# Transformer kernel of split products: an operand's high part first, two norms reordered, a copy moved ahead of a split, the experts' end rotated and halved

## The chip, the cores and the metric

The kernel runs on one core of a Trainium2 chip. The metric is the time of the device for one execution, in microseconds; the shown time is the median of three runs. Everything is float32 data.

## What is computed

Two transformer blocks run over 256 positions of width 1024. The first has a convolution and gated linear attention mixer and a convolutional MLP. The second has two layers: stick-breaking and "fox" attention with a SwiGLU of 2816 columns, then sliding-window attention with a mixture of eight experts, top two of eight for each position. Each of the two layers ends with a gated embedding term. Cut to the parts that the change touches:

```python
x = x + rmsnorm(mixer(rmsnorm(x, g0)), g1)          # w_in ... w_out
h = rmsnorm(x, g2)                                  # two norms in a row after w_out
x = x + rmsnorm(conv_mlp(h), g3)                    # w_up, w_down
x = layer_norm(ALPHA * x + fox_sb_mixer(x))         # ab_in, ab_out
x = layer_norm(ALPHA * x + swiglu(x))               # ffn_up, ffn_down
x = x + sigmoid(x @ ple_gate[0]) * (p[0] @ ple_proj[0])
x = layer_norm(ALPHA * x + swa_mixer(x))            # qkv, c_out
combine = top2_softmax(x @ router_w + router_b)
y = sum(combine[:, e] * swiglu_e(x) for e in range(8))   # 44 weight chunks for each expert
x = layer_norm(ALPHA * x + y)
x = x + sigmoid(x @ ple_gate[1]) * (p[1] @ ple_proj[1])
```

## The kernel before

All five engines follow programs written out by hand, tied by counting semaphores. PE (TensorE) multiplies, ACT (ScalarE) and DVE (VectorE) prepare operands, SP issues the weight loads, POOL some small loads.

**Split products.** A float32 product is made of three: high times high, high times low, low times high. A weight chunk of 128 rows x 2048 columns is loaded to `w_raw`; ACT rounds it to `w_hi` (L611), DVE subtracts to `w_lo` (L1138, in the experts L1701). `w_hi` and `w_lo` have four slots (`RING`). `round_to(c)` on ACT and DVE does all chunks up to number c, so its place in a program sets when a chunk is made. PE waits for `lo_ready` before a chunk and reports `w_used` after it.

**Operands.** Between two projections `operand(m, src)` on PE turns the new activations: it waits for `t_source` of tile 0 (128 positions), makes eight transposes (L1996), then the same for tile 1. ACT rounds each half tile to `xt_hi`, DVE subtracts to `xt_lo` (L1150). Between the steps PE multiplies constants (`keep_warm`, L2001), whose results nobody reads. Their numbers stand in tables; after tile 1 there are seven, and then PE waits for all four pieces of `xt_lo`:

```python
                if m not in (6, 10):
                    keep_warm(7, 3)
                pe.wait_ge(S("xt_ready"), 4 * (m + 1))
```

`cols_chunk` (L1976 to L1979) and `rows_chunk` (L1922 to L1924) then make the three products of each 128 rows of a chunk, one after the other. `operand` serves w_up (m = 2), ab_in (3), ffn_up (5), qkv (7) and the router (9).

**After w_out.** Two norms follow each other: `rms_after` (L1210 to L1218) adds to x, `rms_before` (L1187 to L1195) makes y for w_up. Both go tile by tile: both norms of tile 0, then both of tile 1. ACT takes the squares, the roots, and the `xt_hi` copies in the same order.

**Sliding-window attention.** For each of eight pairs of heads, PE turns the weights, DVE copies them out (`turned_prob`, L1449), PE multiplies by the values (`swa_pv`, L2413 to L2415). Ahead of the last copy DVE splits a weight chunk of c_out (`round_to(c_sw + 7)`) and two pieces of `xt_lo`.

**Experts.** `item(i)` runs expert i: 28 chunks up, 16 down, the latter in two halves of 512 columns (n = 0, 1). ACT and DVE make `ys_hi`, `ys_lo` of a half (L1759), PE's `scatter` (L2485, eight products) puts both halves back to the positions at the start of the next item, and DVE adds them to y (`added`, L1716, a tile of 1024 columns each). The programs of ACT and DVE run two chunks ahead of PE, and end an item with the first four chunks of the next; behind the last expert these are the four chunks of the last embedding term (ple1: two of 1024 columns, which these instructions treat as 2048, and two of 2048). Only then each engine tests whether more than eight items are needed (`overflow`, a nest of `If`); here eight are. DVE then adds, takes the statistics (L1892) and normalizes (L1234 to L1241) tile 0, and PE turns it.

## Time and profile before

| what | value |
|---|---|
| median of three runs (range) | 1875.41 us (1875.24 to 1876.05) |
| profiled execution, its own time | 1876.83 us |
| its span, first to last instruction | 1874.7 us |
| PE busy / DVE busy / ACT busy | 97% / 74% / 59% |
| chain that ended last: PE / DVE / ACT | 87% / 7% / 2% |
| mean granted clock of TensorE | 0.991 |

The span holds the stages w_in to w_down (up to 341 us), the first layer of the second block (to 708), qkv and its attention (to 786), c_out and the router (to 822), the eight experts (to 1826) and the last embedding term. PE's busy share counts the constant products too, so an idle PE is only a part of what a late operand costs: what counts is when the first product with data starts.

### The profile page before, as it was taken

The numbers are of one execution on the slowest core, as the hardware profiler recorded it, in microseconds if no ns is written. First come the engines' busy times: TensorE is split into PE (matmuls) and PEld (weight loads), VectorE is DVE, ScalarE is ACT, GpSimd is POOL, SyncE is SP. The second block draws the span as 40 slices with busy tenths as digits, with TensorE's granted clock in tenths as the row PEclk, the third lists the DMA queues.
The fourth block names the chain that finished last, engine by engine and source line by source line (L and its number), as shares of the span: only waits on it lengthen the run. The fifth ranks groups of instructions, "written<-read, shape, count | busy, mean of one in ns | idle before, by whom it ended". The sixth has DMA issues, their size and how long they took to land.

```text
span 1874.7 us, 24092 instructions
## 1 busy us (share of the span) xinstructions
PE 1827.1 (97%) x9840; PEld 1527.8 (81%) x9849; DVE 1388.8 (74%) x1200; ACT 1105.0 (59%) x989; POOL 61.6 (3%) x83
## 2 busy tenths in 40 slices
PE   8999999999999999999999999999999999999997
PEld 6979997897899877768788888888888888888875
DVE  4766775456655565689988888888888888888876
ACT  4544554364343344367766676767666767676672
POOL 2200000200000001000000000000000000000000
PEclk8999999999999999999999999999999999999998
DMA  7444546432555563259999999999999999999980
GB/s 252 158 153 157 179 157 213 141 131 100 176 179 179 179 203 136 69 205 384 339 381 361 338 368 352 362 356 342 377 361 340 366 355 362 356 342 379 357 308 24
DMA packets 248857, 491.02 MB, mean 262 GB/s; under 512 B 10423, under 2 KB 15611, under 8 KB 248753
## 3 DMA queue, kind: packets, MB, share of 16 engines
q1 hardware_dynamic: 244992, 477.30, 72.0%
q0 software_dynamic: 3328, 10.73, 1.7%
q8 instruction: 69, 1.13, 0.3%
q10 hardware_dynamic: 432, 1.57, 0.2%
q14 instruction: 36, 0.29, 0.0%
HBM read 487.46 MB, written 2.10 MB: 261 GB/s over the span
## 4 chain that ended last, share of the span: by engine, by line
PE 87%; DVE 7%; ACT 2%; issue 1%; DVEq 1%; DMA 0%; ACTq 0%; SPq 0%
PE psum L2511 17%; PE psum L2513 17%; PE psum L2512 17%; PE psum L1976 5%; PE psum L1979 5%; PE psum L1978 5%; PE psum L1922 5%; PE psum L1923 5%; PE psum L1924 5%; PE psum L1996 3%; DVE w_lo L1138 2%; ACT w_hi L611 1%; DVE w_lo L1701 1%; DVE uv L1398 1%; PE psum L2485 1%
## 5 line engine op out<-in xcount | busy, mean ns | idle before, releaser
L611 ACT ACTIVATE w_hi<-w_raw 128x2048 fp32r<-128x2048 f32 (+1 forms) x357 | 641.4, 1834 | 106.7 <-PE psum L1924 60.3
L1701 DVE TENSOR_TENSOR w_lo<-w_raw,w_hi 128x2048 fp32r<-128x2048 f32 (+1 forms) x238 | 511.3, 2187 | 75.2 <-ACT w_hi L611 75.0
L1138 DVE TENSOR_TENSOR w_lo<-w_raw,w_hi 128x2048 fp32r<-128x2048 f32 (+2 forms) x119 | 261.3, 2227 | 138.9 <-ACT w_hi L611 137.5
L2511 PE MATMUL psum<-w_hi,xg_hi 128*128 128x512 f32 x892 | 357.7, 401 | 1.3 <-DVE w_lo L1701 1.3
L2513 PE MATMUL psum<-w_hi,xg_lo 128*128 128x512 f32 x892 | 353.5, 396 | 0.0
L2512 PE MATMUL psum<-w_lo,xg_hi 128*128 128x512 f32 x892 | 353.5, 396 | 0.0
L1701 DVE TENSOR_TENSOR w_lo<-raw_more,w_hi 128x2048 fp32r<-128x2048 f32 (+1 forms) x118 | 254.5, 2195 | 35.2 <-ACT w_hi L611 35.0
L1976 PE MATMUL psum<-xt_hi,w_hi 128*128 128x256 f32 (+1 forms) x976 | 277.0, 284 | 0.7 <-DVE w_lo L1138 0.7
L1978 PE MATMUL psum<-xt_lo,w_hi 128*128 128x256 f32 (+1 forms) x976 | 274.8, 282 | 0.0
L1979 PE MATMUL psum<-xt_hi,w_lo 128*128 128x256 f32 (+1 forms) x976 | 274.8, 282 | 0.0
L611 ACT ACTIVATE w_hi<-raw_more 128x2048 fp32r<-128x2048 f32 (+1 forms) x118 | 212.7, 1838 | 19.0 <-PE psum L2513 18.5
L2511 PEld LDWEIGHTS psum<-w_hi,xg_hi 128*128 128x128 f32 x892 | 168.1, 188 | 40.9 <-DVE w_lo L1701 2.2
L2513 PEld LDWEIGHTS psum<-w_hi,xg_lo 128*128 128x128 f32 x892 | 167.9, 188 | 40.8
L2512 PEld LDWEIGHTS psum<-w_lo,xg_hi 128*128 128x128 f32 x892 | 168.2, 189 | 38.5
L1976 PEld LDWEIGHTS psum<-xt_hi,w_hi 128*128 128x128 f32 (+1 forms) x976 | 181.8, 186 | 3.5 <-DVE w_lo L1138 1.5
L1978 PEld LDWEIGHTS psum<-xt_lo,w_hi 128*128 128x128 f32 (+1 forms) x976 | 182.6, 187 | 0.5
L1979 PEld LDWEIGHTS psum<-xt_hi,w_lo 128*128 128x128 f32 (+1 forms) x976 | 182.6, 187 | 0.3
L2511 PE MATMUL psum<-w_hi,mh_hi 128*128 128x512 f32 x448 | 179.1, 400 | 0.0
L2513 PE MATMUL psum<-w_hi,mh_lo 128*128 128x512 f32 x448 | 177.6, 397 | 0.0
L2512 PE MATMUL psum<-w_lo,mh_hi 128*128 128x512 f32 x448 | 177.4, 396 | 0.0
L611 ACT ACTIVATE mg<-psum 128x512 f32<-128x512 f32 x56 | 33.6, 599 | 176.1 <-PE psum L2513 176.1
L1922 PE MATMUL psum<-w_hi,xt_hi 128*128 128x512 f32 (+1 forms) x256 | 104.5, 408 | 5.2 <-DVE xt_lo L1150 3.7
(395 smaller groups left out, 2122.9 us busy)
## 6 DMA issues: line engine op xcount, KB each, us to landing
w_raw<-in_moe_w_gate_up SPq DMA_DIRECT2D x150, 1024.0 KB, 7.8
raw_more<-in_moe_w_gate_up SPq DMA_DIRECT2D x74, 1024.0 KB, 7.7
w_raw<-in_moe_w_down SPq DMA_DIRECT2D x64, 1024.0 KB, 7.2
raw_more<-in_moe_w_down SPq DMA_DIRECT2D x32, 1024.0 KB, 7.5
w_raw<-in_w_up SPq DMA_DIRECT2D x22, 1024.0 KB, 5.4
w_raw<-in_ffn_w_gate_up SPq DMA_DIRECT2D x22, 1024.0 KB, 5.4
w_raw<-in_w_in SPq DMA_DIRECT2D x12, 1024.0 KB, 5.6
w_raw<-in_ab_w_in SPq DMA_DIRECT2D x12, 1024.0 KB, 5.2
```

What stands on the lines that cost most here:

```text
L611: return act.activation(o, i, func, **kw)
L1138: TT(w_lo[:, k % RING, 0:n], raw(slot, n), w_hi[:, k % RING, 0:n].bitcast(F32), ALU.subtract)\
L1701: TT(w_lo[:, at, 0:n], raw(slot, n), w_hi[:, at, 0:n].bitcast(F32), ALU.subtract).then_inc(S("lo_ready"), 1)
L1922: mm(o, hi(k, t), wh, start=(k == ps[0][0]), stop=False)
L1923: mm(o, hi(k, t), wl, start=False, stop=False)
L1924: m = mm(o, lo(k, t), wh, start=False, stop=(k == kmax))
L1976: mm(o, w_hi[:, slot, cols], xt_hi[:, k, :], start=(k == 0 and c_ % 2 == 0), stop=False, skip_group_check=True)
L1978: mm(o, w_hi[:, slot, cols], xt_lo[:, k, :], start=False, stop=False, skip_group_check=True)
L1979: m = mm(o, w_lo[:, slot, cols], xt_hi[:, k, :], start=False, stop=(k == KD - 1), skip_group_check=True)
L2511: mm(o, hi[:, q, :], wh, start=(q == first), stop=False)
L2512: mm(o, hi[:, q, :], wl, start=False, stop=False)
L2513: m = mm(o, lo[:, q, :], wh, start=False, stop=(q == last))
```

## The change

- `operand` makes two constant products behind tile 1 instead of seven and no longer waits for `xt_lo`. The first chunk of the projection behind it multiplies the high part first (`cols_chunk_high_first` for w_up, ab_in and ffn_up, `rows_operand_high_first` for qkv, the router's loop likewise), and waits for `xt_lo` before the last third. For this the router's scores and the turned embedding of layer 0 (`p_bank`) use other banks.
- After w_out, ACT and DVE do the first norm of both tiles, then the second norm of both. Between the two tiles PE makes 5 constant products, not 14.
- In the attention, the last `turned_prob` stands ahead of the split of the c_out chunk, and the next split moves behind `attended`.
- `item` is cut into `item_head` and `item_end`. Behind the last expert the test for more items comes ahead of the four ple1 chunks on ACT and DVE. `scatter` and `added` go by halves of columns, not by tiles: PE puts half 0 back ahead of the test, half 1 behind it; seven constant products there go, and six in ple1. DVE makes only the two 1024-column chunks ahead of the sum, the other two later.
- `ple(1)` uses `rows_high_first`: both chunks' products with `w_hi` for tile 0, then the turning of tile 1, then those with `w_lo`.

```diff
-            return psum[:, 2 * (phase["c_out"][0][0] % 2), :] if i else scr[:, 3, :]
+            return psum[:, 2 * (phase[("ab_out", "c_out")[i]][1 - i][0] % 2), :]
+        def logit_bank():
+            return psum[0:N_EXP, 2 * (phase["c_out"][1][0] % 2), 0:SEQ]
...
             for t in squares("w_out"):
-                if t == 1:
-                    for j in range(2):
-                        turned(2, j)
                 root_tile(t)
+            for t in range(NT):
                 square_x(t, y, lambda t: act.wait_ge(S("x_tile"), t + 1))
                 root_tile(t)
+            for j in range(2):
+                turned(2, j)
...
+                end = MOE_UP_CHUNKS + len(MOE_DOWN)
+                rounds(k, end + 2, i)
+                wait_used(act, c0 + end, r)
+                item_rows(0)
+                rounds(end + 2, MOE_CHUNKS, i)
+            def item_rows(n):
+                copy(ys_hi[:, n * NB:(n + 1) * NB], psum[:, 4 + n, :], scale=gslot[:, 0:1]).then_inc(S("ys_hi_ready"), 1)
+            def item_end(i):
+                rounds(MOE_CHUNKS, MOE_CHUNKS + 2, i)
+                wait_used(act, N_BEFORE_MOE, (i + 1) * R_ITEM)
+                item_rows(1)
+                rounds(MOE_CHUNKS + 2, MOE_CHUNKS + 4, i)
+            def last_end():
+                c0 = chunk0["ple1"]
+                round_to(c0 + 2, n_items * R_ITEM)
+                wait_used(act, N_BEFORE_MOE, n_items * R_ITEM)
+                item_rows(1)
+                round_to(c0 + 4, n_items * R_ITEM)
...
                 n_items = act.value_load(route_i[0:1, 3:4], min_val=N_EXP, max_val=ITEMS)
-                for i in range(1, N_EXP):
+                n_over = act.value_load(route_i[0:1, 4:5], min_val=0, max_val=ITEMS - N_EXP)
+                for i in range(1, N_EXP - 1):
                     item(i)
+                item_head(N_EXP - 1)
                 def overflow(i):
                     with act.If(n_items > i):
-                        item(i)
+                        item_end(i - 1)
+                        item_head(i)
                         if i + 1 < ITEMS:
                             overflow(i + 1)
                     act.end_ifs()
                 overflow(N_EXP)
                 me.cap = N_STATIC
+                last_end()
                 root_tile(0)
             if "ple1" in live:
...
             for t in rms_after(1, "w_out", "x_tile"):
+                pass
+            for t in range(NT):
                 rms_before(t, 2)
             dve.sem_inc(S("gain_used"), 1)
...
                 if i:
-                    round_to(blocks[0][1] + RING, r)
                     turned(m, 0)
                     turned(m, 1)
                     normalize(1, m, y)
                     dve.sem_inc(S("gain_used"), 2)
+                    round_to(blocks[0][1] + 3, r)
                     turned(m, 2)
                     turned(m, 3)
+                    round_to(blocks[0][1] + 4, r)
                 else:
                     round_to(blocks[0][1] + 4, r)
                     turned(m, 2)
...
                 turned_prob(6)
                 swa_sink(1)
-                round_to(c_sw + 7)
                 for t in range(NT):
                     turned_at(8, t, 2 * t, scr[:, t, :])
                 turned_prob(7)
-                round_to(c_sw + 8)
+                round_to(c_sw + 7)
                 attended(1)
                 for t in range(NT):
...
-            def added(n, t):
-                dve.wait_ge(S("scattered"), 2 * n + t)
-                TT(y[:, t, :], y[:, t, :], psum[:, 4 + 2 * t:6 + 2 * t, :].rearrange("p b n -> p (b n)"), ALU.add)\
-                    .then_inc(S("y_added"), 1)
+            def added(n, h, tiles=range(NT)):
+                dve.wait_ge(S("scattered"), 2 * n + h)
+                cols = slice(h * NB, (h + 1) * NB)
+                for t in tiles:
+                    i = TT(y[:, t, cols], y[:, t, cols], psum[:, 4 + 2 * t + h, :], ALU.add)
+                return i
             def scattered(n):
-                for t in range(NT):
-                    added(n, t)
+                for h in range(2):
+                    added(n, h).then_inc(S("y_added"), 1)
+            def add_last(t):
+                added(n_items, 1, (t,))
+                dve.bn_stats(bn[:, t, 0, :], y[:, t, 0:NB])
+                dve.drain()
+                dve.bn_stats(bn[:, t, 1, :], y[:, t, NB:D])
             def item(i, first=False):
+                item_head(i, first)
+                item_end(i)
+            def item_head(i, first=False):
...
+            def last_end():
+                round_to(chunk0["ple1"] + 2, n_items * R_ITEM)
+                dve.wait_ge(S("ys_hi_ready"), 2 * n_items)
+                item_rows(1)
...
+                last_end()
+                added(n_items, 0)
+                dve.drain()
                 add_last(0)
                 normalize(0, 10, y)
                 add_last(1)
...
+            def cols_chunk_high_first(bl, i, r, m_):
+                bb, cc, n0, n, ps = bl
+                k0, nk, _ = ps[i]
+                slot = (cc + i) % RING
+                pe.wait_ge(S("lo_ready"), RING + cc + i + 1 + RING * r)
+                pe.wait_ge(S("xt_hi_ready"), 4 * m_ + (3 if k0 + nk <= 4 else 4))
+                for part in range(2):
+                    if part:
+                        pe.wait_ge(S("xt_ready"), 4 * (m_ + 1))
+                    for kk in range(nk):
+                        k = k0 + kk
+                        for c_ in range(-(-n // P)):
+                            w_ = min(P, n - c_ * P)
+                            cols = slice(kk * n + c_ * P, kk * n + c_ * P + w_)
+                            o = acc_t(bb % 2, c_)[0:w_, :]
+                            if part:
+                                m = mm(o, w_hi[:, slot, cols], xt_lo[:, k, :], start=False, stop=(k == KD - 1), skip_group_check=True)
+                            else:
+                                mm(o, w_hi[:, slot, cols], xt_hi[:, k, :], start=(k == 0 and c_ % 2 == 0), stop=False,
+                                   skip_group_check=True)
+                                mm(o, w_lo[:, slot, cols], xt_hi[:, k, :], start=False, stop=False, skip_group_check=True)
+                m.then_inc(S("w_used"), 1)
...
-            BETWEEN = (0, 4, 14, 9, 4, 13, 4, 2, 4, 11, 4)
+            BETWEEN = (0, 4, 5, 9, 4, 13, 4, 2, 4, 11, 4)
...
-                if m not in (6, 10):
-                    keep_warm(7, 3)
-                pe.wait_ge(S("xt_ready"), 4 * (m + 1))
+                keep_warm(2, 3)
...
-            def up(blocks, r):
-                for b_ in blocks:
+            def up(blocks, r, m=2):
+                products_t(blocks[0], r, m)
+                if m == 5:
+                    pe.wait_ge(S("ppt_ready"), 1)
+                for b_ in blocks[1:]:
...
-                for b_ in (ks_b, qs_b):
-                    products_t(b_, 0)
+                products_t(ks_b, 0, 3)
+                products_t(qs_b, 0)
...
+                high(0, 0)
+                high(1, 0)
+                turn_tile(m, src, 1)
+                low(0, 0)
+                pe.wait_ge(S("xt_ready"), 4 * m + 4)
+                high(0, 1)
+                high(1, 1)
+                low(0, 1).then_inc(S("w_used"), 1)
+                low(1, 0)
+                low(1, 1).then_inc(S("w_used"), 1)
...
-                    pe.wait_ge(S("y_added"), 2 * n_items + 2)
-                    keep_warm(6)
...
-                products(kv_b, 0, xh, xl)
+                wait_acc(kv_b[0])
+                rows_operand_high_first(kv_b, 7)
...
-            def scatter(n):
-                pe.wait_ge(S("ys_ready"), 2 * n)
-                for t in range(NT):
-                    for h in range(2):
-                        for q, part in enumerate((ys_hi, ys_lo)):
-                            m = mm(psum[:, 4 + 2 * t + h, :], selt[:, t * P:(t + 1) * P], part[:, h * NB:(h + 1) * NB],
-                                   start=(q == 0), stop=(q == 1))
-                    m.then_inc(S("scattered"), 1)
+            def scatter(n, h):
+                pe.wait_ge(S("ys_ready"), 2 * n - 1 + h)
+                for t in range(NT):
+                    for q, part in enumerate((ys_hi, ys_lo)):
+                        m = mm(psum[:, 4 + 2 * t + h, :], selt[:, t * P:(t + 1) * P], part[:, h * NB:(h + 1) * NB],
+                               start=(q == 0), stop=(q == 1))
+                m.then_inc(S("scattered"), 1)
...
+                o = logit_bank()
                 for k in range(KD):
-                    o = scr[0:N_EXP, 0, 0:SEQ]
+                    if k % 4 == 0:
+                        pe.wait_ge(S("xt_hi_ready"), 4 * 9 + 3 + k // 4)
                     mm(o, rw_hi[:, k, :], xt_hi[:, k, :], start=(k == 0), stop=False)
-                    mm(o, rw_hi[:, k, :], xt_lo[:, k, :], start=False, stop=False)
-                    m = mm(o, rw_lo[:, k, :], xt_hi[:, k, :], start=False, stop=(k == KD - 1))
+                    mm(o, rw_lo[:, k, :], xt_hi[:, k, :], start=False, stop=False)
+                pe.wait_ge(S("xt_ready"), 4 * 9 + 4)
+                for k in range(KD):
+                    m = mm(o, rw_hi[:, k, :], xt_lo[:, k, :], start=False, stop=(k == KD - 1))
...
-                keep_warm(7, 0)
-                scatter(N_EXP)
+                scatter(N_EXP, 0)
                 def overflow(i):
                     with pe.If(n_items > i):
                         item(i)
+                        scatter(i + 1, 0)
                         if i + 1 < ITEMS:
                             overflow(i + 1)
-                        if i == N_EXP:
-                            scatter(n_items)
                     pe.end_ifs()
                 overflow(N_EXP)
+                scatter(n_items, 1)
             if "ple1" in live:
```

DVE around the two norms after w_out (x is written by the first norm, y by the second). Before:

```order
L1218 SCALAR_TENSOR_TENSOR x<-y,stat,x 128x1024
L1187 TENSOR_SCALAR stat<-stat 128x1
L1178 RECIPROCAL stat<-stat 128x1
L1195 SCALAR_TENSOR_TENSOR y<-x,stat,gain 128x1024
L1210 TENSOR_TENSOR stat<-stat 128x1
L1187 TENSOR_SCALAR stat<-stat 128x1
L1214 TENSOR_TENSOR y<-psum,gain 128x512
L1178 RECIPROCAL stat<-stat 128x1
L1218 SCALAR_TENSOR_TENSOR x<-y,stat,x 128x1024
```

and now:

```order
L1245 SCALAR_TENSOR_TENSOR x<-y,stat,x 128x1024
L1237 TENSOR_TENSOR stat<-stat 128x1
L1214 TENSOR_SCALAR stat<-stat 128x1
L1241 TENSOR_TENSOR y<-psum,gain 128x512
L1205 RECIPROCAL stat<-stat 128x1
L1245 SCALAR_TENSOR_TENSOR x<-y,stat,x 128x1024
L1214 TENSOR_SCALAR stat<-stat 128x1
L1205 RECIPROCAL stat<-stat 128x1
L1222 SCALAR_TENSOR_TENSOR y<-x,stat,gain 128x1024
```

The first y of the second norm now stands behind both x.

DVE at the end of the attention (`pt` is the turned pair of heads, its last two copies are shown). Before:

```order
L1449 COPY pt_124<-psum 128x768
L1443 TENSOR_TENSOR smx_131<-smx_131,sink 128x16
L1138 TENSOR_TENSOR w_lo<-w_raw,w_hi 128x2048
L1157 TENSOR_TENSOR xt_lo<-psum,xt_hi 128x4x128 x2
L1449 COPY pt_124<-psum 128x768
L1138 TENSOR_TENSOR w_lo<-w_raw,w_hi 128x2048
```

and now:

```order
L1478 COPY pt_124<-psum 128x768
L1472 TENSOR_TENSOR smx_131<-smx_131,sink 128x16
L1184 TENSOR_TENSOR xt_lo<-psum,xt_hi 128x4x128 x2
L1478 COPY pt_124<-psum 128x768
L1165 TENSOR_TENSOR w_lo<-w_raw,w_hi 128x2048
```

The split has moved behind the copy.

DVE behind the last expert, from the last row of the item that runs at the end of the nest (the branch skips the bodies for items nine to eleven). Before:

```order
L1759 SCALAR_TENSOR_TENSOR ys_lo<-psum,gslot,ys_hi 128x512
L1701 TENSOR_TENSOR w_lo<-w_raw,w_hi 128x2048 x2
L1878 UNCONDITIONAL_BRANCH
L1715 REGISTER_ALU
L1716 TENSOR_TENSOR y<-y,psum 128x1024
L1892 BN_STATS bn<-y 128x6 x2
```

and now:

```order
L1937 UNCONDITIONAL_BRANCH
L1163 ISA
L1165 TENSOR_TENSOR w_lo<-raw_more,w_hi 128x1024
L1163 REGISTER_ALU
L1165 TENSOR_TENSOR w_lo<-raw_more,w_hi 128x1024
L1818 REGISTER_ALU
L1804 SCALAR_TENSOR_TENSOR ys_lo<-psum,gslot,ys_hi 128x512
L1747 TENSOR_TENSOR y<-y,psum 128x512 x2
L1744 REGISTER_ALU
L1747 TENSOR_TENSOR y<-y,psum 128x512
L1758 BN_STATS bn<-y 128x6
```

The branch now stands ahead of the last `ys_lo`, and two narrow splits are left between it and the sum.

## Rows read from the trace of the kernel before

**Rows 1.** What PE waited for, whole span: us in total, times, longest

```profile
PE psum L1996 <- DVEq L1242: 12.0, 5, 8.0
```

**Rows 2.** Experts' stretch: us, busy of PE, PEld, DVE, ACT, POOL; clock, DMA share, GB/s

```profile
1100.00:1800.00 700.00, 700.00 (x3136) 566.79 (x3135) 603.51 (x396) 488.85 (x355) 5.68 (x6) 1.00 1.00 357
```

**Rows 3.** Timeline, norms after w_out: start us, us, engine, line, instruction, count, idle before

```profile
130.62 0.40 PE L1924 MATMUL psum<-w_hi,xt_lo 128*128 128x512 f32 x1
...
138.47 0.15 DVE L1187 TENSOR_SCALAR stat<-stat 128x1 f32<-128x1 f32 x1 [1.27 <-ACTq L697]
...
140.53 1.97 PE L1996 MATMUL psum<-ident,y 128*128 128x128 f32 x8 [2.65 <-DVEq L1196]
...
144.35 0.47 PE L1976 MATMUL psum<-xt_hi,w_hi 128*128 128x256 f32 x1
```

**Rows 4.** Timeline, norm after w_down and operand of ab_in

```profile
342.43 0.16 DVE L1210 TENSOR_TENSOR stat<-stat 128x1 f32<-128x1 f32 x1 [1.57 <-ACTq L676]
...
345.15 1.09 PE L1996 MATMUL psum<-ident,x 128*128 128x128 f32 x8 [0.69 <-DVEq L1219]
...
346.08 1.67 PE L2001 MATMUL psum<-ones_tri 128*128 128x512 bf16 x7
...
347.83 0.39 PE L1976 MATMUL psum<-xt_hi,w_hi 128*128 128x256 f32 x1
```

**Rows 5.** Timeline, operand and scores of the router

```profile
811.18 0.28 PE L2575 MATMUL psum<-xt_hi,rw_hi 128*8 128x256 f32 x1 [0.20 <-DVE xt_lo L1150]
...
811.99 2.29 DVE L1811 TENSOR_TENSOR xn_lo<-x,xn_hi 128x2048 fp32r<-128x2048 f32 x1 [0.17 <-ACT xn_hi L611]
...
814.95 0.17 DVE L1815 TENSOR_TENSOR route<-psum,rb_row 128x16 f32<-128x16 f32 x1 [0.67 <-PE psum L2581]
```

**Rows 6.** Timeline, last pairs of the attention, DVE and PE

```profile
770.50 2.29 DVE L1138 TENSOR_TENSOR w_lo<-w_raw,w_hi 128x2048 fp32r<-128x2048 f32 x1
772.71 1.28 DVE L1157 TENSOR_TENSOR xt_lo<-psum,xt_hi 128x512 fp32r<-128x512 f32 x2
773.91 0.95 DVE L1449 COPY pt<-psum 128x768 f32<-128x768 f32 x1
...
774.91 0.43 PE L2413 MATMUL psum<-p,pt 128*128 128x64 f32 x2 [2.34 <-DVE pt L1449]
```

**Rows 7.** Stretch behind that wait: columns as in rows 2

```profile
775.24:778.65 3.41, 3.41 (x14) 3.13 (x14) 3.13 (x5) 0.21 (x1) 0.00 (x0) 0.50 0.73 252
```

**Rows 8.** Timeline, experts' end and last term, PE

```profile
1822.13 0.39 PE L2513 MATMUL psum<-w_hi,mh_lo 128*128 128x512 f32 x1
...
1828.08 0.50 PE L1922 MATMUL psum<-w_hi,ppt_hi 128*128 128x512 f32 x1 [1.89 <-issue]
...
1841.93 1.97 PE L1996 MATMUL psum<-ident,x 128*128 128x128 f32 x8 [7.98 <-DVEq L1242]
...
1845.96 0.93 PE L1922 MATMUL psum<-w_hi,xt_hi 128*128 128x512 f32 x1
```

**Rows 9.** The same stretch, DVE

```profile
1809.82 6.76 DVE L1701 TENSOR_TENSOR w_lo<-w_raw,w_hi 128x2048 fp32r<-128x2048 f32 x4
1823.28 0.75 DVE L1759 SCALAR_TENSOR_TENSOR ys_lo<-psum,gslot,ys_hi 128x512 fp32r<-128x512 f32 x1 [6.71 <-ACT ys_hi L611]
...
1835.88 1.22 DVE L1716 TENSOR_TENSOR y<-y,psum 128x1024 f32<-128x1024 f32 x1 [3.05 <-issue]
...
1843.35 1.29 DVE L1892 BATCH_NORM_STATS2 bn<-y 128x6 f32<-128x512 f32 x2
```

**Rows 10.** Last block of 48 products (ple1): columns as in rows 2

```profile
1858.90:1870.13 11.23, 11.23 (x48) 8.67 (x47) 4.07 (x6) 1.69 (x3) 0.00 (x0) 1.00 0.19 71
```

**Rows 11.** Timeline, first item's opening chunk, whose products have high parts first

```profile
822.72 0.39 PE L2499 MATMUL psum<-w_lo,xg_hi 128*128 128x512 f32 x1
822.95 0.39 PE L2498 MATMUL psum<-w_hi,xg_hi 128*128 128x512 f32 x1
```

**Rows 12.** Page, costliest groups: a weight load of the 256-column products

```profile
L1976 PEld LDWEIGHTS psum<-xt_hi,w_hi 128*128 128x128 f32 (+1 forms) x976 | 181.8, 186 | 3.5 <-DVE w_lo L1138 1.5
```

123 lines of the change are left out of this document (76 added, 47 removed).

## The prediction

> **What bounds the kernel now.** I read the page's busy shares first, then the stretches of the experts, PE's waits, and last the timeline at each hand-over that the diff names. In the experts PE is busy for all of 700 us [rows 2]: it is the bound there, though the DMA engines are full too (share 1.00). Outside, PE's idle time is mostly a wait for the end of a norm: five times, 12.0 us, one of them 8.0 [rows 1]. What ends those waits is DVE's program order, and PE's constant products hide more of them than the busy share tells. So each part of the change is worth what it moves the first product with data forward, and nothing elsewhere. After each hand-over the order of the work is as before, so what is won stays won if PE is the bound behind it.
>
> **Five operands.** Behind tile 1 of ab_in's operand the turning starts at 345.15, seven constant products follow at 346.08 (1.67 us, 0.24 each), and the first product of data starts at 347.83 [rows 4]. With two constant products PE is through at 346.08 + 0.48 = 346.56. The third `xt_hi` piece is there at about 346.45 (0.7 of turning and 0.6 of copy after 345.15), so the start moves to 346.6: **1.2 us**. The high part of the first chunk is 32 products of 0.12 (a 256-column product; the router's follow at that distance), 3.8 us, and covers the rest of `xt_lo`. For ffn_up and qkv the pattern repeats: 1.2 each, 3.6 for the three; bounds 1.0 to 1.3 each. The five constants fewer cost nothing, since work takes their place at once.
>
> At the router the scores come about 1.3 earlier, but DVE is making `xn_lo` from 811.99 to 814.28 and used them at 814.95 [rows 5]. Only 814.95 - 814.28 = 0.67 is left: **0.6** (bounds 0 and 1.3).
>
> **Two norms after w_out.** w_out's products end at 131.0, y of tile 1 is turned at 140.53, w_up starts at 144.35 [rows 3]. New chain: square of tile 1 at once and on to DVE 0.8 (half of the 1.27 that the 1024-column square takes, [rows 3], and a drain); its first norm 2.7 (342.43 to 345.15, [rows 4]); x is complete at 134.5. Then the second norm of tile 0 and of tile 1, 2.06 each (138.47 to 140.53, [rows 3]): turnings possible at 136.6 and 138.6. But PE has only eight constants behind w_out, to about 133.4, and now waits 3.2 us where it waited 0.6. Before this change an idle stretch of 2.65 ahead of 140.53 left the turning at half speed (1.97 for eight transposes against 1.09, [rows 3, 4]). I expect that here: turning of tile 0 takes 1.9, five constants at half speed 2.1, so tile 1 is turned at about 140.5, as before, but at the full clock, and the high part starts 1.45 later, at 141.95. Gain **2.4**. At the full clock throughout it would be 4.0, with the low clock lasting on 0.5: these are the bounds.
>
> **Copy ahead of the split.** `swa_pv` of the last pair waits 2.34 for its copy, because DVE first makes `w_lo` (2.29) and `xt_lo` (1.28) [rows 6]. Without the split `xt_lo` can begin when ACT's pieces are there, about 771.4; it ends at 772.7, the copy at 773.7: 1.2 earlier. The second effect is the larger: behind the wait TensorE ran at the granted clock 0.50, its 1.2 GHz level, in two slices of 3.41, with PE busy throughout; the first is shown [rows 7]. At 1.00 the same work takes 3.4 us less. The idle stretch shrinks to 1.2 us; the longer one of 1.89 behind the experts was followed by 24 products in 5.87, at full speed [rows 8]. The moved split is done at 776.0, ahead of its use; y of tile 0 follows at 777.3, when PE gets there; I take 0.2 for a wait on tile 1. **4.4**, bounds 1.2 (clock falls still) and 4.6.
>
> **Experts' end.** Now: last expert product at 1822.13, eight put-back products, the jump over the unused items with 1.89 idle, 24 products to 1833.95, then 7.98 idle to 1841.93 [rows 8]. DVE meanwhile makes four splits, jumps (3.05), and adds at 1835.88 [rows 9]. New, step by step:
> - DVE ends the experts' splits at 1816.58 and then had nothing until `ys_lo` at 1823.28, 6.7 us [rows 9]. The jump (3.05) and two narrow splits (1.2 each, half of the wide ones) take 5.5 and fit.
> - PE: half 0 put back by 1823.5, jump 1.89, half 1 from 1825.4 to 1826.5. `ys_lo` is ready at 1824.03 [rows 9].
> - DVE adds half 1 of tile 0 at 1826.5. From the sum's start to the turning took 1841.93 - 1835.88 = 6.05; the half-width add is 0.6 shorter: 1832.0. PE is through its 24 products (5.87 from 1826.4) at 1832.2. Turning at 1832.1, **9.8 earlier**.
> - Turning to first gate product took 4.03 [rows 8]. DVE now: add 0.65, statistics 1.3 [rows 9], two `xt_lo` 1.3 [rows 6], drains: 3.4. Start 1835.5.
> - Then 96 products at 11.23 / 48 = 0.234 [rows 10] are 22.5, turning tile 1 is 1.0. DVE has x of tile 1 at 1835.5 + 3.4 = 1838.9 and its split `w_lo` at 1841.2; PE is through 16 high products and the turning at 1840.3 and waits 0.9; `xt_lo` at 1842.5 costs 0.3 more. Last product ends at 1860.3 instead of 1870.13: 9.8; I take **9.7**. Bounds 6 (two new waits each 1 us longer, and the clock low for a while after the 2.2 idle ahead of 1835.5) and 10.5.
>
> `added` by halves in items 2 to 8 makes four instructions of two: some 0.3 more DVE an item. DVE is busy 604 of 700 [rows 2], so PE's time covers it; without that cover it would be 2 us. The extra waits inside w_up's and ffn_up's loops are always met: 0.
>
> **Sum.** 3.6 + 0.6 + 2.4 + 4.4 + 9.7 = 20.7 us. The profiled execution of 1876.83 becomes 1856.1 (span 1874.7 to 1854.0); the median stands 1.4 lower: 1875.4 - 20.7 = **1854.7**.
>
> **Rivals.**
> - *The clock falls at the new idle places* (before tile 0 of w_up, 1.2 in the attention, 2.2 in ple1). For it: the 2.34 wait did that. Against: the 1.89 of the jump did not [rows 8]. Price: 3.2 in the attention, 1.9 in ple1, 1.2 in w_up: 1861.0. Chance 0.12.
> - *The jump becomes a longer wait.* DVE's now falls where the DMA engines still carry ple1's loads; before they were idle. The place has 1.2 us of room (1823.28) and 1.4 more before PE needs `ys_lo`. If it took 8 us instead of 3.05, `scatter` of half 1 would be 2.3 late: 1857.0. Chance 0.04. The Trainium skill (Runtime: NRT & Kernel Launch, Instruction fetch mechanics) says that a taken branch outside the fetched pages stalls for a DMA fetch of its target; by that rule the stall stands in the chain wherever the jump stands, and the two gaps of 1.89 and 3.05 agree.
> - *The experts eat what is won before them*, since the DMA engines are full there [rows 2]: then the 11.0 us of the first four parts are lost, 1865.7. Against: PE is busy 700 of 700 there, and in ACT's waits of that stretch PE stands as the releaser, never a load. Chance 0.04.
> - *Slower: the order of the parts costs.* In 14 chunks (6 of w_up, 6 of ffn_up, ab_in, qkv) `w_hi` and `w_lo` alternate in 32 products each. If such a pair were set by its weight loads, 186 ns [rows 12] instead of 120, that is 448 x 0.066 = 30 us: 1884. It decides from 46 ns a product on. Against: loads are issued for every product already, and the first item's opening chunk, which alternates likewise, runs at 0.23 [rows 11], as all 512-column products do. The Trainium skill (TensorE: Matmul & The Clock Gate, Back-to-back issue gap) says that the spacing in a real stream is set by both weight load and product, which speaks for this rival; no row here shows it for 256 columns alternating. Chance 0.03.
> - *It does little*: several new waits take the places of the old ones at once, within 4 us of before. Chance 0.03.
>
> **Numbers.** The forecast has 0.74. A change under 0.2% (3.8 us) can't be told from none. Faster by more: 0.74 + 0.12 + 0.04 + 0.04 = 0.94; same 0.03; slower 0.03. Range: all bounds on the good side give 1851, the clock rival 1861, all bounds on the bad side 1864.7; I take 1850 to 1864, which leaves out the last two rivals and most of the third.
>
> **What would show it.** First product of w_up near 142, of the others 1.2 nearer to their turnings; no 0.50 stretch near 775, and the 2.34 wait at 1.2; turning of x in ple1 at about 1821 on the new axis (1832 less the 11 won before it), with DVE's jump ahead of its `ys_lo`; a last block of 48 products still 11.2 long. I am wrong if the 7.98 wait persists, if DVE's split is what PE waits for in ple1 by more than 2 us, or if the products of a first chunk stand over 0.13 apart.

## The result and the profile after

The changed kernel took **1857.5 us** (median of four: 1853.9 to 1857.9) against 1875.7 before: a ratio of 0.990 (95% 0.988 to 0.991). Forecast were 1854.7 and a range of 1850 to 1864; 18.2 us were won where 20.7 were forecast. The profiled execution is the fastest of the four, 1853.9 with a span of 1852.2: 22.5 less than the span before. Two of the eleven executions of the run att_only took 3674 and 4587 us and are left out as slow; all other times here are of fast executions. So the sum has two questions: where the profiled execution won more than forecast, and why three of four executions won 3.6 less than it.

The stages of the two traces, each from the first product of a stage to that of the next (us won against the profiled execution of before; the last column is the sum):

```
                 start  w_out  w_down  ab_in  ffn_up  qkv   att   router  experts  end    sum
forecast          0      2.4     0      1.2    1.2    1.2   4.4    0.6      0      9.7   20.7
changed kernel    0.86   1.56    1.54   1.25   1.31   1.56  4.43   0.75    -0.07   9.29  22.54
```

(Gaps of up to 0.06 lie between stages. The profiled execution of before took 1876.8, about one more than its medians of 1875.6 to 1876.0, so the sums of these rows are about one more than what two medians differ by.) Every stage has the sign forecast. Two columns stood in no step: `start`, and `w_down`, in which the change edits nothing.

The hand-over behind w_out in the changed kernel, PE's and DVE's timeline (start us, us, engine, line, instruction, count, idle before and what ended it):

```profile
130.63 1.67 PE L2099 MATMUL psum<-ones_tri 128*128 128x512 bf16 x7 [0.16 <-issue]
135.87 1.97 PE L2094 MATMUL psum<-ident,y 128*128 128x128 f32 x8 [3.56 <-DVEq L1223]
137.62 2.34 PE L2099 MATMUL psum<-ones_tri 128*128 128x512 bf16 x5
139.76 1.91 PE L2094 MATMUL psum<-ident,y 128*128 128x128 f32 x8
141.47 0.80 PE L2099 MATMUL psum<-ones_tri 128*128 128x512 bf16 x2
141.91 0.47 PE L2054 MATMUL psum<-xt_hi,w_hi 128*128 128x256 f32 x1
```

```profile
134.50 1.28 DVE L1222 SCALAR_TENSOR_TENSOR y<-x,stat,gain 128x1024 f32<-128x1024 f32 x1
...
136.60 1.28 DVE L1222 SCALAR_TENSOR_TENSOR y<-x,stat,gain 128x1024 f32<-128x1024 f32 x1
```

DVE has `y` of tile 1 at 137.9, 2.6 ahead of the turning in [rows 3] (0.9 of it is the start), but PE turns it only at 139.76. Both turnings and the five constant products ("constants" from here on) between them run at half speed: the granted clock is 0.50 from 135.03, within the idle stretch of 3.56, to 141.86.

The operand of ab_in and then of qkv: two constants where seven stood ([rows 4]), and the first product 1.4 and 1.2 behind the start of the turning:

```profile
341.20 1.09 PE L2094 MATMUL psum<-ident,x 128*128 128x128 f32 x8 [0.69 <-DVEq L1246]
342.13 0.59 PE L2099 MATMUL psum<-ones_tri 128*128 128x512 bf16 x2
342.63 0.36 PE L2054 MATMUL psum<-xt_hi,w_hi 128*128 128x256 f32 x1
342.83 0.28 PE L2056 MATMUL psum<-xt_hi,w_lo 128*128 128x256 f32 x1
342.95 0.28 PE L2054 MATMUL psum<-xt_hi,w_hi 128*128 128x256 f32 x1
...
703.72 1.09 PE L2094 MATMUL psum<-ident,x 128*128 128x128 f32 x8 [0.91 <-DVEq L1654]
...
704.90 0.47 PE L1993 MATMUL psum<-w_hi,xt_hi 128*128 128x256 f32 x1
```

`w_hi` and `w_lo` alternate at 0.12 a product. The last pair of the attention, answering [rows 6]: its wait is 1.05 instead of 2.34.

```profile
765.47 0.43 PE L2542 MATMUL psum<-p,pt 128*128 128x64 f32 x2 [1.05 <-DVE pt L1478]
...
766.84 0.48 PE L1976 MATMUL psum<-w_hi,xt_hi 128*128 128x512 f32 x1
767.15 0.40 PE L1977 MATMUL psum<-w_lo,xt_hi 128*128 128x512 f32 x1
```

The experts' end, PE and then DVE, answering [rows 8, 9]. The 7.98 wait is gone; what stands in the chain now is 2.13 of the jump, 2.32 for `xt_lo` and 0.98 for `w_lo`.

```profile
1808.89 0.39 PE L2642 MATMUL psum<-w_hi,mh_lo 128*128 128x512 f32 x1
...
1812.32 0.49 PE L2614 MATMUL psum<-ys_hi,selt 128*128 128x512 f32 x1 [2.13 <-issue]
...
1819.05 1.09 PE L2094 MATMUL psum<-ident,x 128*128 128x128 f32 x8
1822.46 0.49 PE L2442 MATMUL psum<-w_hi,xt_hi 128*128 128x512 f32 x1 [2.32 <-DVE xt_lo L1177]
...
1826.31 1.04 PE L2094 MATMUL psum<-ident,x 128*128 128x128 f32 x8
1828.33 1.20 PE L2449 MATMUL psum<-w_lo,xt_hi 128*128 128x512 f32 x4 [0.98 <-DVE w_lo L1165]
```

```profile
1808.12 2.36 DVE L1165 TENSOR_TENSOR w_lo<-raw_more,w_hi 128x1024 fp32r<-128x1024 f32 x2 [4.78 <-ACT w_hi L615]
1810.40 0.74 DVE L1804 SCALAR_TENSOR_TENSOR ys_lo<-psum,gslot,ys_hi 128x512 fp32r<-128x512 f32 x1
...
1813.54 0.69 DVE L1747 TENSOR_TENSOR y<-y,psum 128x512 f32<-128x512 f32 x1 [1.21 <-PE psum L2614]
```

From the last expert product to the end of PE's work it is 38.7 us instead of 48.0. The experts are as long as before: PE busy 700.00 of 700 us, DVE 605 against 604 of [rows 2].

```profile
1100.00:1800.00 700.00, 700.00 (x3131) 566.55 (x3131) 604.96 (x406) 491.00 (x353) 5.66 (x6) 1.00 0.99 355
```

At the router `xn_lo` (2.29) still ends last, as [rows 5] had it. Two microseconds later stands a wait that I had not looked for:

```profile
799.43 2.29 DVE L1868 TENSOR_TENSOR xn_lo<-x,xn_hi 128x2048 fp32r<-128x2048 f32 x1 [0.17 <-ACT xn_hi L615]
801.63 0.17 DVE L1872 TENSOR_TENSOR route<-psum,rb_row 128x16 f32<-128x16 f32 x1
```

```profile
800.89 1.90 PE L2099 MATMUL psum<-ones_tri 128*128 128x512 bf16 x7
803.60 0.39 PE L2721 MATMUL psum<-route,tri_excl 128*128 128x8 f32 x2 [0.81 <-DVEq L1889]
```

The scores' turning comes 1.3 earlier and DVE's choice of experts 0.75 earlier, so PE's eight constants between them end too soon. In the kernel before, the same place reads:

```profile
816.92 0.39 PE L2587 MATMUL psum<-route,tri_excl 128*128 128x8 f32 x2 [0.25 <-DVEq L1832]
```

### The profile page after: what moved, and what is told of

It reads as the page before. It is cut to its first block, busy times and chain, and to the rows that moved or that the text cites. A ratio compares the mean times of both kernels' runs of the same rounds, so it can differ in the third digit from the quotient of the medians.

```text
span 1852.2 us, 24041 instructions
## 1 busy us (share of the span) xinstructions
PE 1809.8 (98%) x9795; PEld 1518.7 (82%) x9802; DVE 1388.4 (75%) x1217; ACT 1103.5 (60%) x989; POOL 61.0 (3%) x83
## 4 chain that ended last, share of the span: by engine, by line
PE 88%; DVE 7%; ACT 2%; issue 1%; DVEq 1%; DMA 0%; ACTq 0%; SPq 0%
PE psum L2640 16%; PE psum L2642 16%; PE psum L2641 16%; PE psum L1976 5%; PE psum L1978 5%; PE psum L1977 5%; PE psum L2071 4%; PE psum L2074 4%; PE psum L2073 4%; PE psum L2094 3%; DVE w_lo L1165 2%; DVE w_lo L1730 1%; ACT w_hi L615 1%; PE psum L2054 1%; PE psum L2052 1%
## 5 line engine op out<-in xcount | busy, mean ns | idle before, releaser
L1165 DVE TENSOR_TENSOR w_lo<-w_raw,w_hi 128x2048 fp32r<-128x2048 f32 (+2 forms) x121 | 265.7, 2228 | 135.2 <-ACT w_hi L615 133.6
L1730 DVE TENSOR_TENSOR w_lo<-raw_more,w_hi 128x2048 fp32r<-128x2048 f32 (+1 forms) x116 | 250.1, 2195 | 34.8 <-ACT w_hi L615 34.5
L2071 PE MATMUL psum<-xt_hi,w_hi 128*128 128x256 f32 (+2 forms) x768 | 217.6, 283 | 0.7 <-DVE w_lo L1165 0.7
L2074 PE MATMUL psum<-xt_hi,w_lo 128*128 128x256 f32 (+2 forms) x768 | 216.9, 282 | 0.0
L2073 PE MATMUL psum<-xt_lo,w_hi 128*128 128x256 f32 (+2 forms) x768 | 215.9, 281 | 0.0
L2071 PEld LDWEIGHTS psum<-xt_hi,w_hi 128*128 128x128 f32 (+2 forms) x768 | 143.2, 186 | 2.8 <-DVE w_lo L1165 1.5
L2073 PEld LDWEIGHTS psum<-xt_lo,w_hi 128*128 128x128 f32 (+2 forms) x768 | 143.8, 187 | 0.5
L2074 PEld LDWEIGHTS psum<-xt_hi,w_lo 128*128 128x128 f32 (+2 forms) x768 | 142.5, 186 | 0.3
L2642 PEld LDWEIGHTS psum<-w_hi,mh_lo 128*128 128x128 f32 x448 | 84.4, 188 | 20.6
```

The source lines that it names most:

```text
L1165: TT(w_lo[:, k % RING, 0:n], raw(slot, n), w_hi[:, k % RING, 0:n].bitcast(F32), ALU.subtract)\
L1730: TT(w_lo[:, at, 0:n], raw(slot, n), w_hi[:, at, 0:n].bitcast(F32), ALU.subtract).then_inc(S("lo_ready"), 1)
L2071: mm(o, w_hi[:, slot, cols], xt_hi[:, k, :], start=(k == 0 and c_ % 2 == 0), stop=False, skip_group_check=True)
L2073: mm(o, w_hi[:, slot, cols], xt_lo[:, k, :], start=False, stop=False, skip_group_check=True)
L2074: m = mm(o, w_lo[:, slot, cols], xt_hi[:, k, :], start=False, stop=(k == KD - 1), skip_group_check=True)
L2642: m = mm(o, lo[:, q, :], wh, start=False, stop=(q == last))
```

## The experiments

Two theories stood at the start. **A**: each part is worth what its hand-over moves, as in the sum. **B**: the waits that the change leaves let the granted clock fall in most executions, and that is the missing 3.6. The first runs gave a narrower one, **C**: the place is the router's new wait. Times are medians. The runs stand in three groups, each on a chip of its own and beside runs of the kernel before on that chip (1876.0, 1875.6 and 1875.8): after_again, no_end, att_only and ops_undone in the first; router_warm, router_undone, wout_warm and all_warm in the second; att_warm, norms_undone_w, after_third and two_warm in the third. Which chip gave the first result is not on record.

### The changed kernel again

No edit.

> The changed kernel itself, nothing edited, to see what its two groups of times (1853.9 once, 1857.5 to 1857.9 three times) are. Theory A (the sum: every part is worth what its hand-over moves): the median is 1857.5 within 0.5 and the profile has the same places as the first. Theory B (the clock: the waits that the change leaves, 3.6 behind w_out, 1.1 before the last swa_pv, 2.3 in ple1, let TensorE's granted clock fall to 0.50 in most executions): an execution of 1857.5 has a mean granted clock of 0.990 to 0.991 and shows 15 to 20 us more at 0.50 than that of 1853.9, at one or more of these three places, with PE busy in it for about 7 us (3.6 lost).

1855.2 (four executions), ratio 0.989 (0.988 to 0.991). The executions: 1853.0 and 1853.3 at a mean clock of 0.994, 1857.1 and 1857.5 at 0.991. So the executions fall into two kinds, a lower and an upper group of times, and they differ in the clock. The profile is of the lower one, so it can't show what B expects of the upper; its stages, with those of a later repeat (after_third):

```
                 start  w_out  w_down  ab_in  ffn_up  qkv   att   router  experts  end    sum
again             0.85   3.05    1.52   1.25   1.31   1.57  4.43   0.76    -0.06   8.74  23.44
after_third       0.61   2.99    1.53   1.25   1.30   1.49  4.43   0.75    -0.07   8.70  23.05
```

All columns repeat within 0.1 but three: `start`, `w_out` and `end`, and in the last two the difference is a stretch at 0.50 that is longer, shorter or absent.

### The experts' end undone

```diff
-                last_end()
+                me.chunk += RING
-                scatter(N_EXP, 0)
+                keep_warm(7, 0)
+                scatter(N_EXP)
...
```

(and the sums by tiles, ple1's order and the head and end of an item, all as before).

> The changed kernel with the experts' end as it was (put-back whole behind the jump, sums by tiles, ple1 in its old order), all other parts kept. Theory A: the end is worth 9.3 to 9.7, so the median is 1866.8 to 1867.3, and turning of x in ple1 stands 19.8 behind the last expert product as before (1822.13 to 1841.93). Rival (what is won before the experts is lost in them, and the whole gain is the end): the median is above 1873. Theory B: the old end has a stretch at 0.50 of its own (10.2 us behind the 8.0 wait), so undoing the end costs at least 9.3 and the difference from the changed kernel stays near 9.5 only if that one loses its 3.6 elsewhere; if the changed kernel loses them in ple1, the difference is about 6.

1865.8, ratio 0.994 (0.993 to 0.996). Again two groups: 1863.5 and 1863.7 at 0.993 and 0.992, 1865.8 to 1866.6 at 0.989 and 0.990. Group against group the end is worth 10.2 in the lower (1853.4) and 9.0 in the upper (1857.5); 9.3 to 9.7 were expected, which neither meets, and the rival's 1873 is out. This profile is of the upper group, and there the loss is seen. It reaches the route products when the changed kernel does (803.59 against 803.60); from there on:

```profile
803.59 0.39 PE L2642 MATMUL psum<-route,tri_excl 128*128 128x8 f32 x2 [0.87 <-DVEq L1837]
...
805.40 3.18 PE L2518 MATMUL psum<-sel,xn_hi 128*128 128x128 f32 x16
808.37 3.62 PE L2518 MATMUL psum<-sel,xn_lo 128*128 128x128 f32 x16
811.79 0.73 PE L2549 MATMUL psum<-w_hi,xg_hi 128*128 128x512 f32 x1
```

From the first of the 32 gathering products to the first expert product it is 6.4 instead of 3.7. The same 5.12 us of both kernels, by windows (length, busy of PE, PEld, DVE, ACT, POOL, granted clock, DMA share, GB/s), this one first and the changed kernel second:

```profile
806.15:811.27 5.12, 5.12 (x26) 5.12 (x26) 1.46 (x1) 2.66 (x2) 0.00 (x0) 0.50 0.00 0
```

```profile
806.15:811.27 5.12, 5.12 (x38) 4.72 (x37) 3.42 (x3) 3.74 (x3) 0.00 (x0) 1.00 0.14 18
```

The stretch at 0.50 is 10.2 us long. The first expert product comes 1.92 later than before instead of 0.75 earlier: 2.7 lost. That is the fall that theory C names, seen in one trace. Of B's places this trace has the one behind w_out at 0.50 for 3.4 us, as the repeats of the lower group have, and the attention not at all; ple1's new wait is not in this kernel. In the four other traces with the router's wait unfilled (the changed kernel's three and wout_warm's) no fall follows it.

### The attention's part alone, and its clock alone

In the kernel before, DVE's `round_to` moved behind the last copy (att_only), and, in a later group, DVE's order untouched and PE's wait filled instead (att_warm):

```diff
                 swa_turn(7)
+                keep_warm(9, 2 * (q0_b[0] % 2))
                 swa_pv(7)
```

> The kernel before with one part of the change: DVE's wait-and-split ahead of the last copy of swa_pv moved behind it. Theory A with the clock kept: 4.4 faster, 1871.3, the wait of swa_pv on its copy 1.1 instead of 2.34 and no stretch at 0.50 near 775. Theory A with the clock falling still: 1.2 faster, 1874.5. Theory B: between the two and spread over the executions, since a wait of 1.1 lets the clock fall in some.

> The kernel before with nine constant products (2.2 us) in the wait of 2.34 ahead of the last swa_pv, DVE's order untouched. Theory A with its split of the term (1.2 of order, 3.2 of clock): the wait's end stays where it was and the stretch at 0.50 near 775 is gone, 3.2 faster, 1872.6. Rival (all 4.4 are the order, the clock's fall costs nothing since something else ends there): no faster than 1875.4. Rival (constants late by a part of one): 0.2 less.

att_only: 1872.7 over nine executions, ratio 0.998 (0.997 to 0.999); its trace has 4.43 at this stage, to the hundredth what the full change has, no stretch at 0.50 near 775, and 0.45 lost again at the end. att_warm: 1873.6, ratio 0.999 (0.998 to 1.000); its trace has 3.13 at this stage. The products behind the wait, and the stretch of [rows 7]:

```profile
772.57 1.89 PE L2001 MATMUL psum<-ones_tri 128*128 128x512 bf16 x8
774.86 0.43 PE L2413 MATMUL psum<-p,pt 128*128 128x64 f32 x2 [0.40 <-DVE pt L1449]
```

```profile
775.24:778.65 3.41, 3.41 (x22) 2.96 (x22) 3.13 (x5) 0.15 (x1) 0.00 (x0) 1.00 0.80 254
```

The wait ends at 774.86 as before (774.91), and 22 products stand where 14 did. By medians the two runs win 3.2 and 2.2, where 4.4 and 3.2 were expected: each is one short of its stage, as the trace of before is one above its medians. So the term of 4.4 is 3.1 of clock and 1.3 of order, as its working had it (3.4 and 1.2), and the rival by which the clock costs nothing falls.

### The operand's tail undone

```diff
-                keep_warm(2, 3)
+                if m not in (6, 10):
+                    keep_warm(7, 3)
+                pe.wait_ge(S("xt_ready"), 4 * (m + 1))
```

The high part stays first inside the chunks.

> The changed kernel with the end of operand() as before: seven constant products behind the turning and a wait for all of xt_lo, ahead of the four first chunks and the router; the order inside those chunks stays high part first. Theory A: 1.2 slower at ab_in, ffn_up and qkv each, up to 1.3 at w_up, and 0.6 at the router (its wait comes back, without the constants that m = 9 had too): 4.2 to 5.5, so 1862 to 1863. Rival (nothing hangs on this, the first chunk's weights or the next wait end last there): under 1.5. Rival (order costs): the order alone makes it slower than the kernel before would be, so undoing the wait alone brings over 5.5.

1860.8, ratio 0.992 (0.991 to 0.993), all five executions from 1860.5 to 1861.5 at 0.993 to 0.995: no upper group. Against the changed kernel's lower group (1853.4) that is 7.4 slower, more than the 5.5 expected. By stages: ab_in, ffn_up, qkv and the router give nothing any more (-0.02, 0.00, -0.01, -0.01 against 1.25, 1.31, 1.5, 0.75), w_out gives 1.29 instead of 3.0, and 1.54 are lost to a stretch at 0.50 at 685.5, behind a wait of 1.39 that all kernels have. So the whole gain of these places is the two constants and the lifted wait. The 7.4 is over the 5.5 from which the rival of the order's cost was to show, but the excess is mostly this stretch. That the order costs something is out: with the order kept, ab_in and ffn_up stand within 0.02 of the kernel before.

### The router: filled, and undone

```diff
-            WARM = (8, 4)
+            WARM = (11, 4)
```

for router_warm; for router_undone the products in their old order behind seven constants and all of `xt_lo`.

> The changed kernel with 11 constant products instead of 8 between the turned scores and the route products (a wait of 0.81 stands there now, of which 3 x 0.24 = 0.72 is filled). The eight executions of the changed kernel so far: 1853.0, 1853.3, 1853.9 at a mean clock of 0.994 or 0.995, and five from 1857.05 to 1857.9 at 0.990 or 0.991. Theory C (the router part opened a wait of 0.81 in the stretch where TensorE does little else, and the clock then falls for about 10 us in part of the executions): no execution at 0.991 or below, all of 1853.0 to 1854.5. Theory B in its old form (the clock falls at the waits of 3.6, 1.1 or 2.3): nothing changes, about half of the executions stay at 1857.5. Theory A (no matter of the clock): nothing changes.

> The changed kernel with the router's products in the old order, behind seven constant products and all of xt_lo. Theory A: 0.75 slower than the changed kernel in both its groups (1854 and 1858.3). Theory C: 0.75 slower than its fast group, but without the slow one: all executions at 1854 to 1855, so the median is 2 to 3 faster than the changed kernel's median.

router_warm: 1853.8, ratio 0.988 (0.987 to 0.990), 1853.6 to 1854.4 at 0.994 and 0.995: one group. router_undone: 1855.1, ratio 0.989 (0.988 to 0.991), 1854.8 to 1856.2 at 0.994 and 0.995: one group, 1.3 behind router_warm on the same chip, of which 0.76 is the router's stage. Both came as C had it, but they don't decide for C: wout_warm, on this chip too, leaves the router's wait unfilled and has no upper execution either. That the filled wait keeps the upper group away is therefore not shown, and against the repeats of the changed kernel (1855.2 and 1854.4) router_undone is no faster. What the trace of no_end does show is that A's plain reading, a gain of 0.75 at the router, does not hold in every execution: in that one 2.7 are lost against it.

### Constants in the waits

wout_warm has 22 constants behind w_out instead of 8; all_warm has those, 11 at the router, 4 ahead of the last `swa_pv` and 8 ahead of ple1's first gate product; two_warm has only w_out's 22 and the router's 11.

```diff
-            BEFORE = (0, 10, 8, 0, 18, 0, 4, 0, 18, 0, 24)
+            BEFORE = (0, 10, 22, 0, 18, 0, 4, 0, 18, 0, 24)
```

> The changed kernel with 22 constant products behind w_out instead of 8 (14 x 0.24 = 3.4 of the wait of 3.56). Theory A with the clock as the size of this term: the turning of tile 0 takes 1.1 instead of 1.9 to 2.0 and the five constants 1.2 instead of 2.3; tile 1 is turned at 138.3 to 138.6 and w_up starts near 140.0 in every execution: 1.9 faster than the first profile of the changed kernel, 0.4 than the second, in whose place the clock fell for half as long. Rival (the wait does no harm, since DVE's norm of tile 1 ends last): tile 1 is turned at 138.6 or later and under 0.4 is gained. Rival (constants delay the turning): slower by up to 0.5. By theory C the two groups of times persist.

> The changed kernel with constant products in every wait that it opened or left: 22 instead of 8 behind w_out, 4 ahead of the last swa_pv (1.05 of waiting), 11 instead of 8 at the router (0.81), 8 ahead of ple1's first gate product (2.3). Theory C and A with clock together: one group of times, mean clock 0.995 to 0.997, median 1851.5 to 1853, faster than either group of the changed kernel. Rival (constants get in the way of the first products with data): slower than 1853.3 by up to 1, one group all the same. If only the wait behind w_out counted, two groups stay.

> The changed kernel with constants in two of the four waits only: 22 behind w_out, 11 at the router. Theory C with the clock's share at w_out: one group, 1852.2 to 1853.2, since the waits of 1.05 in the attention never showed a fall and that of 2.3 in ple1 starts with the jump's 2.13, in which no constants stand. Rival (ple1's constants carry a part of the 1.6 between 1853.8 and 1852.2): 1852.9 or more, clock of 0.995 to 0.996, and a stretch at 0.50 near 1812 in the profile.

wout_warm: 1852.9, ratio 0.988 (0.986 to 0.989), four executions from 1852.1 to 1854.9 at 0.994 to 0.997, though the router's wait stands in it: here C's two groups were expected and did not come. Its profile is of the execution of 1854.9. Behind w_out it is as good as all_warm's (its `w_out` column too is 4.2), but its start is 0.5 later than all_warm's, its end stage 8.68, and the clock falls behind the wait of 1.39 that all kernels have, for 1.56 lost:

```profile
680.39:683.80 3.41, 3.41 (x9) 2.63 (x10) 3.41 (x4) 3.39 (x3) 0.00 (x0) 0.50 0.99 258
```

all_warm: 1852.2, ratio 0.988 (0.986 to 0.989), 1852.1 to 1852.7. two_warm: 1852.3, ratio 0.988 (0.986 to 0.989), one of its four at 1854.7, where one group was expected. The stages:

```
                 start  w_out  w_down  ab_in  ffn_up  qkv   att   router  experts  end    sum
all_warm          0.06   4.21    1.52   1.27   1.31   1.49  4.42   0.75    -0.05   9.24  24.26
two_warm         -0.02   4.17    1.52   1.27   1.30   1.50  4.43   0.75    -0.05   9.29  24.21
router_warm       0.42   2.80    1.53   1.27   1.31   1.48  4.42   0.75    -0.06   8.21  22.17
norms_undone_w    0.52   2.51    1.53   1.25   1.31   1.48  4.42   0.75    -0.06   8.74  22.48
```

all_warm behind w_out (the view begins at 133, so its first row counts only the last 15 of the 22):

```profile
132.72 3.40 PE L2099 MATMUL psum<-ones_tri 128*128 128x512 bf16 x15
136.66 1.09 PE L2094 MATMUL psum<-ident,y 128*128 128x128 f32 x8 [0.53 <-DVEq L1223]
137.59 1.24 PE L2099 MATMUL psum<-ones_tri 128*128 128x512 bf16 x5
138.76 1.09 PE L2094 MATMUL psum<-ident,y 128*128 128x128 f32 x8
139.69 0.59 PE L2099 MATMUL psum<-ones_tri 128*128 128x512 bf16 x2
140.19 0.36 PE L2054 MATMUL psum<-xt_hi,w_hi 128*128 128x256 f32 x1
```

The turnings stand at 136.66 and 138.76, and w_up starts 4.2 earlier than before. Its profile has no stretch at 0.50 between 20.8 and 1850.3. The constants of the attention and of ple1 bring nothing to the median: two_warm, on another chip, does without them. These two beat both kernels, by 23.5 us the one before.

### The norms' order undone

router_warm with root and second norm of tile 0 ahead of the first norm of tile 1 on DVE and ACT, and 14 constants between the tiles, as before (DVE's part is shown):

```diff
             for t in rms_after(1, "w_out", "x_tile"):
-                pass
-            for t in range(NT):
                 rms_before(t, 2)
```

> The changed kernel with 11 constants at the router (one group of times, 1853.8) and the norms behind w_out in their old order: root and second norm of tile 0 before the first norm of tile 1, 14 constants between the tiles; the new tail of the operand stays. Theory A: the term of 2.4 is 1.2 of the operand's tail (as at ab_in) and 1.2 of the order, so 1.2 slower, 1855.0. Theory D (the order gives nothing of its own as long as the clock falls behind the new wait of 3.56: tile 1 was turned at 139.85, 0.7 before the 140.53 of the kernel before, of which 0.4 is the start): within 0.4 of 1853.8. With tile 1 turned at about 140.1 and the clock kept, it is even.

1854.4, ratio 0.989 (0.987 to 0.991), 0.6 behind router_warm, with one execution in four at 1856.8. In the traces the stage differs by 0.3 (2.51 against 2.80). The time lies between D's 0.4 and A's 1.2, on another chip than router_warm; the stage is D's, and so is tile 1's turning, expected at about 140.1 with the clock kept:

```profile
140.01 1.09 PE L2092 MATMUL psum<-ident,y 128*128 128x128 f32 x8 [2.65 <-DVEq L1223]
...
141.44 0.36 PE L2052 MATMUL psum<-xt_hi,w_hi 128*128 128x256 f32 x1
```

The old order turns tile 1 at 140.01 at full speed; the new one is ready 2 us sooner and turns it at 139.85 (router_warm), with the turning of tile 0 and the constants slowed. This trace had the better of the clock: in the kernel before the clock fell at the same wait of 2.65 ([rows 3], 1.97 for the turning). Against this trace the reordering is worth 1.7 with w_out's constants (4.2).

### How often the clock falls

> The changed kernel once more, unedited: how often an execution falls into its upper group. So far five of eight, against none of seventeen in the kernels where constants stand in the router's wait of 0.81 or in that behind w_out. Theory C: two groups again, 1853 to 1854 at a clock of 0.994 or more and 1857 to 1858 at 0.991 or less, nothing between; if the profiled execution is of the upper group, it shows 10 us at 0.50 from about 805 on, with about 2.7 lost there. Rival (chance of the session): one group only.

1854.4, ratio 0.989 (0.987 to 0.990), 1853.4, 1854.3, 1854.6 and 1856.5, all at 0.993 to 0.995: C expected two groups here, and none of the four is in the upper one by its clock; the rival, one group only, came. Counted over all: where the router's wait of 0.8 stands unfilled (the changed kernel thrice, no_end, wout_warm), 8 of 21 executions are of the upper group; where it is filled or undone (six kernels), 0 of 25. But the 8 are all of the first result and of the first chip of the experiments. On that chip it is 5 of 9 unfilled against 0 of 5 (ops_undone alone, which moves other stages too); on the other two chips it is 0 of 8 unfilled against 0 of 20. So the chip or the session is a rival of C that these counts can't rule out: a filled and an unfilled kernel side by side where the upper group does come was not run.

## Why the prediction was right, and where it was not

The direction, the time (2.8 off) and the range came out; the sum's steps fared unequally.

- **Five operands, 3.6 + 0.6.** Measured 1.25, 1.31 and 1.5 to 1.6, and 0.75 at the router: right, qkv undersized by 0.3. The pieces are confirmed stage by stage by the run without the tail.
- **Two norms after w_out, 2.4 (0.5 to 4.0).** 1.56, 3.05 and 2.99 in three traces of the same kernel, 4.2 with constants. Ready times (136.6 and 138.6), idle stretch (3.2; it is 3.56) and a tile 1 turned no earlier than before came as worked out. What varies is how long the clock stays low: in the profiled execution through the second turning too (1.91 instead of 1.09), so the high part started at 142.8 on the old axis and not at 141.95. By parts, the operand's tail is 1.6 in the new order (2.9 less the 1.29 without it) and 1.9 in the old one (2.51 of norms_undone_w less 0.59, which att_only has here with the old order and tail, since its clock did not fall). The reordering by itself is left with 0.3 to 0.7 (2.80 less 2.51, 1.29 less 0.59).
- **Copy ahead of the split, 4.4.** 4.43 in every trace, 3.1 of it clock and 1.3 order. The part of 0.2 against it was not needed.
- **Experts' end, 9.7.** 9.29; 8.74 and 8.70 in the repeats. The turning came 9.6 earlier (forecast 9.8), from there to the first gate product 3.4 as forecast, the rest 25.1 instead of 24.8. DVE's jump is hidden, PE's is 2.13. What I had not priced at its place: in four of ten traces with the new end the clock falls at or right behind PE's jump, at 1811 to 1814, where the stage is 8.2 to 8.7; in a fifth (router_undone) it falls at 1822.3, and the stage is 8.5. One trace without a fall there (norms_undone_w) has 8.74 too: in it PE's jump takes 2.67 instead of 2.13, which is the difference. One such window, of router_warm:

```profile
1812.02:1815.43 3.41, 3.41 (x9) 2.67 (x10) 1.62 (x4) 2.15 (x2) 0.00 (x0) 0.50 0.06 16
```

- **w_down, 0.** Missing from the sum, 1.5 in the profile. In the kernel before PE waits 2.75 at 289.28 and then runs slow; in the changed one the same wait stands at 286.87 and the clock stays:

```profile
290.54:293.95 3.41, 3.41 (x10) 2.65 (x9) 3.41 (x3) 0.74 (x1) 0.00 (x0) 0.50 0.93 330
```

```profile
286.87:290.28 3.41, 3.41 (x15) 2.77 (x16) 3.41 (x2) 2.00 (x2) 0.00 (x0) 1.00 0.62 216
```

All three traces with the old operand tail at w_up and the old norms have this fall, none of the eleven with the change (the runs without the tail and without the norms' order among them) has it. No kernel was made to find which edit moves it.
- **Rivals.** "The clock falls at the new idle places" is the nearest to what came, in part of the executions, at little more than half its price (6.3 on top of the sum for three places; the upper group is 3.6 above the profiled execution). Its places were wrong too: the attention's wait of 1.05 never showed it, and the router, where no_end's trace loses 2.7, was not among them. I had costed the router as a gain with a waiting DVE behind it, and did not ask what PE does while DVE is still at `xn_lo`: its eight constants had been counted out for the old distance. "The experts eat it" falls (experts' column -0.05 to -0.08, and -0.21 in no_end, whose low clock reaches into them). "The order costs" falls: 0.12 a product throughout. The Trainium skill (TensorE: Matmul & The Clock Gate, Back-to-back issue gap) would have the spacing set by weight load and product together; for 256 columns with changing weights the trace shows no cost beyond the 0.12. "The jump becomes longer" falls: PE's idle before it is 1.97 to 2.67 in the ten traces (1.89 before), and DVE's lies within an idle of 4.78 that ended with ACT's `w_hi`; the `ys_lo` behind it was done at 1811.1, before PE's 1812.32.

Errors of opposite sign meet in the median. The profiled execution won 1.8 more than the sum: w_down 1.5, the start 0.9, qkv and router 0.5 on top, w_out 0.8 and the end 0.4 short. The upper group then loses 3.6. Of the 4.1 between the groups of the changed kernel, 2.7 is seen in a trace of another kernel (no_end, whose groups lie 2.9 apart). No trace of the changed kernel's upper group exists, so that its loss too lies at the router is inferred, and the remaining 1.4 stay open; so does why wout_warm and after_third had no such execution. One execution in four lies about 2 us above the rest in four kernels. In three of them its clock is the lowest too (0.994 against 0.995 to 0.997 in wout_warm, two_warm and norms_undone_w), and wout_warm's was profiled: the three differences named there are its 2.6 us over all_warm. For after_third (1856.5 at 0.994, like the rest) it stays open.

## What to carry over

When an operation is moved forward, follow the constant products that were measured out for its old distance: here a wait of 0.8 opened at the router, and in one trace the low clock behind it lost 2.7 where the step had won 0.75. Fill the wait that a reordering opens on TensorE in the same edit, or the reordering may pay next to nothing: behind w_out, 14 more products took the stage from between 1.6 and 3.0 to 4.2. (The 3 at the router changed no stage; whether they keep the slower executions away is not shown.) Judge a part of a change by its stage in the trace, but its worth by several executions: most stage columns repeat within 0.1, while executions of the same program lie 4 us apart. And put the two kernels whose groups you count side by side on one chip, where both groups occur.
